# Gated DeltaNet stage: full 128-wide products in the first five merge levels, and decay differences built on VectorE

## The chip, the cores and the metric

The kernel runs on one core of one Trainium2 chip. The metric is the device time of one execution in microseconds (us); a smaller number is better.

## The reference

One layer of a hybrid encoder over two token groups (1024 and 512 tokens, together 1536 tokens in 12 tiles of 128), model width 1024. The part that matters here is the second of three mixers, a bidirectional gated DeltaNet with 4 heads of width 128:

```python
g = jnp.cumsum(g, axis=-1)
decay = jnp.exp(jnp.where(incl, g[..., :, None] - g[..., None, :], -jnp.inf))
k_beta = k * beta[..., None]
a_mat = jnp.einsum("bhnid,bhnjd->bhnij", k_beta, k) * jnp.where(strict, decay, 0.0)
sol = lax.linalg.triangular_solve(eye + a_mat, rhs, left_side=True, lower=True, unit_diagonal=True)
qk = jnp.einsum("bhnid,bhnjd->bhnij", q, k) * decay
...
v_new = u_c - jnp.einsum("bhck,bhkv->bhcv", w_c, s)
s = s * jnp.exp(gl_c)[..., None] + jnp.einsum("bhck,bhcv->bhkv", kd_c, v_new)
```

Both directions are computed. Around it stand an input projection, neighbourhood attention, an RG-LRU, a gated merge and a squared-relu MLP, all in float32.

## The kernel before

`trunk` runs its stages one after another; `deltanet` is one of them. It works through the 4 heads in order. In each head the kernel uses chunks of 128 tokens and handles them in six **units**: `UN` lists them as (token block of four tiles, direction), so a unit is four 128x128 matrices, a tile of 128x512. Every engine has its own program, and they meet only at the named semaphores in `S`. VectorE is `dve`, ScalarE `act`, GpSimd `pool`, TensorE `pe`, SyncE `sp`. A head goes through three parts.

**The decay part.** For each of the six units ScalarE builds two tiles of `dd` from the decay row `gbc` and the per-token column `col` (L1304 to L1315): eight activations of 128x128 (relu of row minus column, and of column minus row), then two exponentials of 128x512. GpSimd multiplies both by a triangular mask (`decays`, L1244). VectorE then turns the Gram products in PSUM into `am` (L1613, four instructions of 128x128) and `qk` (L1616, one of 128x512); before each it scales two tiles to token order (`token_major`, L1625), and twice in a head it multiplies `qd` by the queries (L1638). `dd` has two pairs of tiles, so ScalarE waits before unit n until `amat` of unit n-2 is done. TensorE makes the Gram products of one token block at a time (L1428), and those of the next block wait until VectorE has read those of the last. When the sixth unit is done, TensorE transposes `am` into `at` (L1441).

**The level loop.** The triangular inverse is built by merging diagonal blocks, seven levels (`LEVELS`) over six units. The first level is a masked copy. The other six make 36 steps (`NS`) on TensorE: step s issues the first product of s (S: `at` by `tn`, L1457 or L1460), the second product of s-2 (U: `sbuf_s` by `un`, L1471 or L1474) and a transpose of s-4 (T: L1490). ScalarE copies S out of PSUM (L1336 or L1338) and T (L1326); VectorE merges U under a mask into `un` (L1654). In the first 30 steps, those below `SMALL`, the blocks being merged lie in the two 64-row diagonal quadrants. There each 128x128 product is made as two of 64 columns, one for each quadrant, placed in the array by `tile_position`; the ScalarE copy is in two halves too. The last six steps are full products. Between these steps the engines do the next head's convolution, norms and scaling (`front`, at fixed unit numbers) and the last head's output (`OUT_AT`). The next S of a unit waits for its transposed tile to be copied (`t_ev`), and TensorE keeps program order.

**The chain.** Eight sequential steps over the tokens of a head update the state `st` (L1500 to L1515, L1682 to L1686).

Of the kernel before, what the change touches and what calls it, by code (L numbers as in the profile page):

```python
# [17 lines left out]
ACT = mybir.ActivationFunctionType  # L18
ALU = mybir.AluOpType
AX = mybir.AxisListType  # L20

P = 128
# [4 lines left out]
NT = T // P  # L27
TB = 512
NTB = T // TB
# [1065 lines left out]
NS = UNITS - 2 * NTB  # L1095
# [4 lines left out]
def deltanet(nc, proj, g_rows, cols, masks, o_t, conv_w, norm_w, ident, ones):  # L1100
# [9 lines left out]
    UN = [(tg, d) for tg in range(NTB) for d in range(2)]  # L1110
    with Space(nc, "dn") as s:
# [5 lines left out]
        S = {x: s.sem(x) for x in names}  # L1117
# [16 lines left out]
        nw = s.sb("nw", [1])  # L1134
        col = s.sb("col", [4, NT])
        cx = s.sb("cx", [6, NT])
        ncol = s.sb("ncol", [2, NT])
        ms, rr, rs = (s.sb(v, [2, NT]) for v in ("ms", "rr", "rs"))
        oms, orr, ors = (s.sb(v, [NT]) for v in ("oms", "orr", "ors"))
        st = s.sb("st", [4, P])  # L1140
# [14 lines left out]
        def glast(d):  # L1155
            g4 = gbc[:, d].rearrange("p (t n) -> p t n", n=P)
            return g4[:, :, P - 1] if d == 0 else g4[:, :, 0]

        SMALL = NS - 2 * NTB
        halves = (slice(0, 64), slice(64, P))  # L1160

        def live_chains(step):
            return [(j, d, SEG[g][0] // P + (step if d == 0 else SEG[g][1] // P - 1 - step))
# [103 lines left out]
        def _(act):  # L1267
# [29 lines left out]
            def main(i, more):  # L1297

                act.wait_ge(S["cols_in"], i + 1)
                act.activation(flat(cx[:]), flat(cx[:]), ACT.Exp).then_inc(S["cexp"], 1)  # L1300
                act.wait_ge(S["g_in"], i * 32 + 32)
                for d in range(2):
                    act.activation(qd[:, d], gbc[:, d], ACT.Exp).then_inc(S["eg"], 1)
                for n, (tg, d) in enumerate(UN):  # L1304
                    b = n % 2
                    if n >= 2:
                        act.wait_ge(S["amat"], i * 12 + 2 * (n - 2) + 2)
                    for sign, a, bias in ((1.0, 2 * b, ncol), (-1.0, 2 * b + 1, col)):
                        for j in range(4):
                            t = 4 * tg + j  # L1310
                            act.activation(dd[:, a, j], gbc[:, d, t * P:(t + 1) * P], ACT.Relu, bias=bias[:, d, t:t + 1],
                                           scale=sign).then_inc(S["ediff"], 1)
                    for a in (2 * b, 2 * b + 1):
                        act.wait_ge(S["ediff"], i * 48 + 8 * n + 4 + 4 * (a - 2 * b))
                        act.activation(flat(dd[:, a]), flat(dd[:, a]), ACT.Exp, scale=-1.0).then_inc(S["dexp"], 1)  # L1315

                act.wait_ge(S["scaled"], i * 6 + 6)
                act.copy(kf[:], yn[:, 1]).then_inc(S["kc"], 1)
                for n in range(2 * NTB):
                    act.wait_ge(S["u_mm"], i * VT + n + 1)  # L1320
                    act.copy(at[:, n], ps[:, 4 + 2 * (n % 2)]).then_inc(S["at_ev"], 1)

                def turned(k):

                    act.wait_ge(S["t_mm"], i * NTR + k + 1)
                    act.copy(tn[:, k % 6], ps[:, 4 + 2 * (k % 2)]).then_inc(S["t_ev"], 1)  # L1326

                for k in range(NS):
                    act.wait_ge(S["s_mm"], i * NS + k + 1)
                    if k == 0:  # L1330
                        act.wait_ge(S["amat"], i * 12 + 12)
                    if k >= 4:
                        act.wait_ge(S["u_mm"], i * VT + 6 + k - 3)
                    if k < SMALL:
                        for r in halves:
                            last = act.copy(sbuf_s[k % 4][r, :, r], ps[r, k % 2, :, r])  # L1336
                    else:
                        last = act.copy(sbuf_s[k % 4], ps[:, k % 2])  # L1338
                    last.then_inc(S["s_ev"], 1)
                    if T_LAG <= k < NTR + T_LAG:  # L1340
                        turned(k - T_LAG)
                    u = k + 2 * NTB
                    if i and u == OUT_AT["squares"]:
                        out_squares(i - 1)
                    if i and u == OUT_AT["root"]:
                        out_root(i - 1)
                    if more:
                        front(i + 1, u)
                    if u == ZTANH_AT:
                        act.wait_ge(S["z_in"], i * 16 + 16)  # L1350
                        act.activation(th[:, 1], zt, ACT.Tanh, scale=0.5).then_inc(S["zt"], 1)

                act.wait_ge(S["stored"], i * 16 + 16)
                for step in range(8):
                    for j, d, t in live_chains(step):
                        act.wait_ge(S["new_mm"], i * 24 + K_OF[(step, j)] + 1)
                        if step:
                            act.wait_ge(S["st_mm"], i * 24 + K_OF[(step - 1, j)] + 1)
                        act.copy(nb[:, j], ps[:, 4 + j, 0]).then_inc(S["new_ev"], 1)
                    for j, d, t in live_chains(step):  # L1360
                        act.wait_ge(S["o_mm"], i * 24 + K_OF[(step, j)] + 1)
                        act.copy(oc[d][:, t * P:(t + 1) * P], ps[:, 4 + j, 1]).then_inc(S["o_ev"], 1)
                if not more:
                    out_squares(i)
                    out_root(i)
# [7 lines left out]
        def _(pe):  # L1373
# [29 lines left out]
            def main(i, more):  # L1403
# [40 lines left out]
                for step in range(NS + T_LAG):  # L1444
                    if step < NS:
                        k, n = step, step % 6

                        if k < 6:
                            pe.wait_ge(S["u_ev"], i * VT + k + 1)
                        else:  # L1450
                            pe.wait_ge(S["t_ev"], i * NTR + k - 5)
                        if k >= 2:
                            pe.wait_ge(S["s_ev"], i * NS + k - 1)
                        for j in range(4):
                            if k < SMALL:
                                for r in halves:
                                    last = pe.matmul(ps[r, k % 2, j, r], at[:, n, j, r], tn[:, n, j, r], start=True, stop=True,  # L1457
                                                     tile_position=(0, r.start))
                            else:
                                last = pe.matmul(ps[:, k % 2, j], at[:, n, j], tn[:, n, j], start=True, stop=True)  # L1460
                        last.then_inc(S["s_mm"], 1)
                    if U_LAG <= step < NS + U_LAG:
                        k = step - U_LAG
# [2 lines left out]

                        pe.wait_ge(S["u_ev"], i * VT + 6 + k - 1)
                        for j in range(4):
                            if k < SMALL:
                                for r in halves:  # L1470
                                    last = pe.matmul(ps[r, 5 + 2 * (k % 2), j, r], sbuf_s[k % 4][:, j, r], un[:, n, j, r], start=True,  # L1471
                                                     stop=True, tile_position=(0, r.start))
                            else:
                                last = pe.matmul(ps[:, 5 + 2 * (k % 2), j], sbuf_s[k % 4][:, j], un[:, n, j], start=True, stop=True)  # L1474
                        last.then_inc(S["u_mm"], 1)
                        if i and 6 + k == OUT_AT["lengths"]:
                            out_lengths(i - 1)
# [50 lines left out]
        def _(dve):  # L1528
# [64 lines left out]
            def main(i, more):  # L1593
# [2 lines left out]

                c.link(dve.tensor_copy(col[:], cols[:, bass.ds(i, 1)].rearrange("p a k t -> p (a k) t")))
                dve.wait_ge(S["g_in"], i * 32 + 32)
                c.add(dve.tensor_scalar(ncol[:], col[:, 0:2], -1.0, None, ALU.mult))
                for d in range(2):  # L1600
                    c.add(dve.tensor_copy(cx[:, d], col[:, d]))
                    c.add(dve.tensor_tensor(cx[:, 2 + d], glast(d), col[:, d], ALU.subtract))
# [1 line left out]
                c.wait()  # L1604
                dve.sem_inc(S["cols_in"], 1)

                def amat(n):
                    tg, d = UN[n]
                    b = n % 2
                    dve.wait_ge(S["dmask"], i * 12 + 2 * n + 2)  # L1610
                    dve.wait_ge(S["gram"], i * NTB + tg + 1)
                    for j in range(4):
                        last = dve.scalar_tensor_tensor(am[:, n, j], ps[:, 0, j], col[:, 2 + d, 4 * tg + j:4 * tg + j + 1],  # L1613
                                                        dd[:, 2 * b, j], ALU.mult, ALU.mult)
                    last.then_inc(S["amat"], 1)
                    dve.tensor_tensor(qk[:, n], ps[:, 1], dd[:, 2 * b + 1], ALU.mult).then_inc(S["amat"], 1)  # L1616

                def token_major(n):
# [3 lines left out]
                    for d in range(2):  # L1622
# [2 lines left out]
                        dve.tensor_tensor(dst[:, d, 4 * tg:4 * tg + 4], ps[:, 4 + n % 4], fac.unsqueeze(2).to_broadcast([P, 4, P]),  # L1625
                                          ALU.mult).then_inc(S["kt_ev"], 1)

                dve.wait_ge(S["cexp"], i + 1)

                c.link(dve.scalar_tensor_tensor(cx[:, 0:2], col[:, 2:4], -1.0, cx[:, 0:2], ALU.mult, ALU.mult))  # L1630

                dve.wait_ge(S["scaled"], i * 6 + 6)
                for n in range(2 * NTB):
                    token_major(n)
                    if n % 3 == 1:
                        d = n // 3
                        dve.wait_ge(S["eg"], i * 2 + d + 1)
                        dve.tensor_tensor(qd[:, d], qd[:, d], yn[:, 0], ALU.mult).then_inc(S["qd"], 1)  # L1638
                    amat(n)
# [69 lines left out]
        if _step < SEG[_g][1] // P:  # L1709
            K_OF[(_step, _j)] = len(K_OF)  # L1710
K_FRONT = len(CONV_AT) + 1
K_DN = 1 + 7 + 1


def merge_project(nc, proj, o_t, w_br, w_out, x_tm, under_x, rows):
# [636 lines left out]
```

## Time and profile before

| | |
|---|---|
| runs | 3393.93 us median of 3 (3393.69 to 3394.67) |
| the profiled execution | 3393.69 us |
| its span in the profile | 3391.9 us |
| busy, share of the span | PE 92%, PEld 75%, DVE 37%, ACT 34%, POOL 34% |
| mean granted TensorE clock | 0.953 |
| the DeltaNet stage | about 1245 to 1960 us of the span |

The times of a row are from the start of the span. PE is the matmul side of TensorE and PEld its weight loads, which run beside the matmuls. A float32 matmul shows as two records on each; a transpose shows as one. The start of one group of PEld records to the start of the next is the time in which TensorE issued the group. DVE is VectorE, ACT ScalarE, POOL GpSimd. A granted clock of 1.00 is 2.4 GHz, 0.50 is 1.2 GHz. Busy times overlap a little where an engine pipelines: an instruction's record can end after the next has begun.

### The profile page before, as it was taken

The page shows a single profiled execution, that of the slowest core. Times are in us where ns is not written, and L with a number is a line of the kernel's source. Part 1 is how long each engine was busy: PE and PEld are TensorE (multiplying, and loading weights), DVE is VectorE, ACT ScalarE, POOL GpSimd, SP SyncE. Part 2 cuts the span into 40 slices and gives each one's busy share as a digit, 9 for nine tenths or more (in the row PEclk, how much of TensorE's full clock was granted, in tenths as well). Part 3 has the DMA queues.
Part 4 walks back from the last instruction along what each step waited for, and adds up shares of the span by engine and source line. Part 5 has one row for each costly group of instructions (what it writes and reads, how often), then busy time and mean ns, then how long its engine had stood idle before and what let it go on. Part 6 is the DMA issues. An engine that isn't in the chain of part 4 may idle for free. (4 is left out here: it accounts for less than half of the span.)

```text
span 3391.9 us, 44853 instructions
## 1 busy us (share of the span) xinstructions
PE 3118.0 (92%) x18195; PEld 2556.8 (75%) x18195; DVE 1262.6 (37%) x1955; ACT 1149.6 (34%) x2003; POOL 1167.7 (34%) x761
## 2 busy tenths in 40 slices
PE   6999999999998966969696889998999999999998
PEld 4788887878887544858585768786888888888887
DVE  4242323221100787576755423412223323232323
ACT  3221213141111655565656421223233333333222
POOL 4211111111111202121212034245666666656664
PEclk8999999999999987979797989998999999999999
DMA  3533232433421741001000064433332333323331
GB/s 103 176 134 109 72 106 93 130 101 112 135 87 64 254 134 48 20 29 39 29 20 1 20 204 167 146 120 118 99 94 93 100 100 97 118 84 100 100 124 62
DMA packets 235963, 334.30 MB, mean 99 GB/s; under 512 B 32368, under 2 KB 185712, under 8 KB 235760
## 3 DMA queue, kind: packets, MB, share of 16 engines
q1 hardware_dynamic: 235760, 331.44, 30.4%
q8 instruction: 146, 2.39, 0.3%
q14 instruction: 57, 0.47, 0.0%
HBM read 254.27 MB, written 86.93 MB: 101 GB/s over the span
## 5 line engine op out<-in xcount | busy, mean ns | idle before, releaser
L102 PE MATMUL pj_acc<-u_hi,pj_w_hi 128*128 128x512 f32 x1464 | 583.1, 398 | 15.1 <-POOL u_lo L488 13.3
L104 PE MATMUL pj_acc<-u_hi,pj_w_lo 128*128 128x512 f32 x1464 | 571.8, 391 | 0.0
L103 PE MATMUL pj_acc<-u_lo,pj_w_hi 128*128 128x512 f32 x1464 | 571.7, 390 | 0.0
L2269 DVE TENSOR_TENSOR x_tm<-m_ps,x_tm 128x512 f32<-128x512 f32 x384 | 265.0, 691 | 745.3 <-PE m_ps L104 745.3
L482 POOL TENSOR_TENSOR pj_w_lo<-pj_w_raw,pj_w_hi 128x1024 fp32r<-128x1024 f32 x61 | 148.2, 2430 | 826.7 <-ACT pj_w_hi L512 826.7
L102 PEld LDWEIGHTS pj_acc<-u_hi,pj_w_hi 128*128 128x128 f32 x1464 | 276.0, 188 | 78.3 <-POOL u_lo L488 14.2
L2146 POOL TENSOR_TENSOR m_w_lo<-m_w_raw,m_w_hi 128x1024 fp32r<-128x1024 f32 x96 | 237.9, 2498 | 262.7 <-ACT m_w_hi L2060 262.7
L103 PEld LDWEIGHTS pj_acc<-u_lo,pj_w_hi 128*128 128x128 f32 x1464 | 276.1, 189 | 62.0 <-issue 5.7
L104 PEld LDWEIGHTS pj_acc<-u_hi,pj_w_lo 128*128 128x128 f32 x1464 | 275.8, 188 | 57.7
L102 PE MATMUL m_ps<-m_v_hi,m_w_hi 128*128 128x512 f32 x768 | 300.1, 391 | 2.4 <-DVE m_v_lo L2237 2.4
L103 PE MATMUL m_ps<-m_v_lo,m_w_hi 128*128 128x512 f32 x768 | 299.8, 390 | 0.0
L104 PE MATMUL m_ps<-m_v_hi,m_w_lo 128*128 128x512 f32 x768 | 299.7, 390 | 0.0
L102 PE MATMUL m_ps<-m_w_hi,m_h_hi 128*128 128x512 f32 x768 | 299.5, 390 | 0.0
L104 PE MATMUL m_ps<-m_w_hi,m_h_lo 128*128 128x512 f32 x768 | 298.8, 389 | 0.0
L103 PE MATMUL m_ps<-m_w_lo,m_h_hi 128*128 128x512 f32 x768 | 298.8, 389 | 0.0
L2139 POOL TENSOR_TENSOR m_w_lo<-m_w_raw,m_w_hi 128x1024 fp32r<-128x1024 f32 x96 | 227.6, 2391 | 22.4 <-ACT m_w_hi L2053 22.4
L1878 POOL TENSOR_TENSOR mo_w_lo<-mo_w_raw,mo_w_hi 128x512 fp32r<-128x512 f32 x72 | 94.4, 1310 | 336.9 <-ACT mo_w_hi L1845 336.9
L512 ACT CAST pj_w_hi<-pj_w_raw 128x1024 fp32r<-128x1024 f32 x61 | 64.0, 1049 | 404.7 <-PE pj_acc L104 392.1
L2072 ACT CAST m_h_hi<-m_rel 128x512 fp32r<-128x512 f32 x96 | 59.8, 623 | 356.4 <-POOL m_rel L2152 356.4
L2060 ACT CAST m_w_hi<-m_w_raw 128x1024 fp32r<-128x1024 f32 x96 | 96.4, 1052 | 247.1 <-PE m_ps L104 247.1
L102 PEld LDWEIGHTS m_ps<-m_v_hi,m_w_hi 128*128 128x128 f32 x768 | 144.8, 189 | 32.9 <-DVE m_v_lo L2237 2.8
L103 PEld LDWEIGHTS m_ps<-m_v_lo,m_w_hi 128*128 128x128 f32 x768 | 144.9, 189 | 30.2
(261 smaller groups left out, 5419.2 us busy)
## 6 DMA issues: line engine op xcount, KB each, us to landing
m_w_raw<-in_w_mlp_dram SPq DMA_DIRECT2D x48, 1024.0 KB, 5.4
m_w_raw<-in_w_mlp_dram SPq DMA_DIRECT2D x96, 512.0 KB, 3.6
proj<-pj_stage SPq DMA_DIRECT2D x61, 768.0 KB, 3.4
pj_w_raw<-in_w_in_dram SPq DMA_DIRECT2D x61, 512.0 KB, 4.7
mo_gate<-proj SPq DMA_DIRECT2D x24, 768.0 KB, 4.3
mo_w_raw<-in_w_out_dram SPq DMA_DIRECT2D x48, 256.0 KB, 2.6
rpb_bias<-pj_shut SPq DMA_DIRECT2D x48, 192.0 KB, 3.0
rpb_bias<-rpb_near SPq DMA_DIRECT2D x24, 384.0 KB
```

The costliest lines, as they stand in the source:

```text
L102: pe.matmul(out, w_hi, x_hi, start=first, stop=False)
L103: pe.matmul(out, w_hi, x_lo, start=False, stop=False)
L104: return pe.matmul(out, w_lo, x_hi, start=False, stop=last)
L482: pool.tensor_tensor(w_lo[:, n % 2], w_raw[:, n % 2], w_hi[:, n % 2].bitcast(F32), ALU.subtract).then_inc(lo_done, 1)
L512: act.copy(w_hi[:, n % 2], w_raw[:, n % 2]).then_inc(hi_done, 1)
L1878: pool.tensor_tensor(w_lo[:, sl % 2], w_raw[:, sl % 3], w_hi[:, sl % 2].bitcast(F32), ALU.subtract).then_inc(w_lo_done, 1)
L2060: act.copy(w2_hi[:, (2 * gg + j) % 4], w2_raw[:, j]).then_inc(w2_hi_done, 1)
L2072: act.copy(h_hi[:, m % 4], rel[:, j]).then_inc(hh_done, 1)
L2139: pool.tensor_tensor(w1_lo[:, m % 4], w1_raw[:, :, j * P:(j + 1) * P], w1_hi[:, m % 4].bitcast(F32), ALU.subtract).then_inc(w1_lo_done, 1)
L2146: pool.tensor_tensor(w2_lo[:, m % 4], w2_raw[:, j], w2_hi[:, m % 4].bitcast(F32), ALU.subtract).then_inc(w2_lo_done, 1)
L2269: dve.tensor_tensor(xt, ps2[:, q % 4], xt, ALU.add).then_inc(added, 1)
```

## The change

Two edits, both in `deltanet`.

The first takes `SMALL` and `halves` away: in the first 30 steps of the level loop S and U are made as full 128x128 products, four for a unit instead of eight of 64 columns, without `tile_position`, and ScalarE copies the whole 128x512 tile in one instruction.

The second moves the decay differences. ScalarE keeps the two exponentials. VectorE gets a function `ediff(n)`: one subtraction of 128x512 (row minus column, broadcast), a minimum with zero into the second tile, a maximum with zero in place in the first. It is called for unit n+1 ahead of `token_major(n)` and `amat(n)`. The first half of `amat` becomes two 128x512 multiplications, the second waiting for the first, where four 128x128 instructions stood. `ncol` goes.

```diff
-                    for sign, a, bias in ((1.0, 2 * b, ncol), (-1.0, 2 * b + 1, col)):
-                        for j in range(4):
-                            t = 4 * tg + j
-                            act.activation(dd[:, a, j], gbc[:, d, t * P:(t + 1) * P], ACT.Relu, bias=bias[:, d, t:t + 1],
-                                           scale=sign).then_inc(S["ediff"], 1)
-                    for a in (2 * b, 2 * b + 1):
-                        act.wait_ge(S["ediff"], i * 48 + 8 * n + 4 + 4 * (a - 2 * b))
-                        act.activation(flat(dd[:, a]), flat(dd[:, a]), ACT.Exp, scale=-1.0).then_inc(S["dexp"], 1)
+                    act.activation(flat(dd[:, 2 * b]), flat(dd[:, 2 * b]), ACT.Exp, scale=-1.0).then_inc(S["dexp"], 1)
+                    act.activation(flat(dd[:, 2 * b + 1]), flat(dd[:, 2 * b + 1]), ACT.Exp).then_inc(S["dexp"], 1)
...
-                    if k < SMALL:
-                        for r in halves:
-                            last = act.copy(sbuf_s[k % 4][r, :, r], ps[r, k % 2, :, r])
-                    else:
-                        last = act.copy(sbuf_s[k % 4], ps[:, k % 2])
-                    last.then_inc(S["s_ev"], 1)
+                    act.copy(sbuf_s[k % 4], ps[:, k % 2]).then_inc(S["s_ev"], 1)
...
-                            if k < SMALL:
-                                for r in halves:
-                                    last = pe.matmul(ps[r, k % 2, j, r], at[:, n, j, r], tn[:, n, j, r], start=True, stop=True,
-                                                     tile_position=(0, r.start))
-                            else:
-                                last = pe.matmul(ps[:, k % 2, j], at[:, n, j], tn[:, n, j], start=True, stop=True)
+                            last = pe.matmul(ps[:, k % 2, j], at[:, n, j], tn[:, n, j], start=True, stop=True)
...
-                            if k < SMALL:
-                                for r in halves:
-                                    last = pe.matmul(ps[r, 5 + 2 * (k % 2), j, r], sbuf_s[k % 4][:, j, r], un[:, n, j, r], start=True,
-                                                     stop=True, tile_position=(0, r.start))
-                            else:
-                                last = pe.matmul(ps[:, 5 + 2 * (k % 2), j], sbuf_s[k % 4][:, j], un[:, n, j], start=True, stop=True)
+                            last = pe.matmul(ps[:, 5 + 2 * (k % 2), j], sbuf_s[k % 4][:, j], un[:, n, j], start=True, stop=True)
...
+                def ediff(n):
+                    tg, d = UN[n]
+                    b = n % 2
+                    if n >= 2:
+                        dve.wait_ge(S["amat"], i * 12 + 2 * (n - 2) + 2)
+                    e = dd[:, 2 * b]
+                    c.link(dve.tensor_tensor(e, four(gbc[:, d, tg * TB:(tg + 1) * TB]),
+                                             col[:, d, 4 * tg:4 * tg + 4].unsqueeze(2).to_broadcast([P, 4, P]), ALU.subtract))
+                    dve.tensor_scalar(dd[:, 2 * b + 1], e, 0.0, None, ALU.min).then_inc(S["ediff"], 1)
+                    dve.wait_ge(S["ediff"], i * 12 + 2 * n + 1)
+                    dve.tensor_scalar(e, e, 0.0, None, ALU.max).then_inc(S["ediff"], 1)
...
-                    for j in range(4):
-                        last = dve.scalar_tensor_tensor(am[:, n, j], ps[:, 0, j], col[:, 2 + d, 4 * tg + j:4 * tg + j + 1],
-                                                        dd[:, 2 * b, j], ALU.mult, ALU.mult)
-                    last.then_inc(S["amat"], 1)
+                    c.link(dve.tensor_tensor(am[:, n], ps[:, 0], dd[:, 2 * b], ALU.mult))
+                    dve.tensor_tensor(am[:, n], am[:, n], col[:, 2 + d, 4 * tg:4 * tg + 4].unsqueeze(2).to_broadcast([P, 4, P]),
+                                      ALU.mult).then_inc(S["amat"], 1)
                     dve.tensor_tensor(qk[:, n], ps[:, 1], dd[:, 2 * b + 1], ALU.mult).then_inc(S["amat"], 1)
...
+                ediff(0)
                 dve.wait_ge(S["cexp"], i + 1)
...
                 for n in range(2 * NTB):
+                    if n + 1 < 2 * NTB:
+                        ediff(n + 1)
                     token_major(n)
```

## Rows read from the trace of the kernel before

**Rows 1.** The page, part 1: busy time of each engine.
```profile
PE 3118.0 (92%) x18195; PEld 2556.8 (75%) x18195; DVE 1262.6 (37%) x1955; ACT 1149.6 (34%) x2003; POOL 1167.7 (34%) x761
```

**Rows 2.** Windows: the 30 narrow level steps of heads 1, 3; sum of all four.
```profile
core 0: us, PE busy (x) PEld busy (x) DVE busy (x) ACT busy (x) POOL busy (x), PEclk, DMA share, GB/s
...
1494.70:1563.80 69.10, 64.67 (x1114) 54.98 (x1115) 53.10 (x66) 50.89 (x99) 6.98 (x2) 0.91 0.20 59
...
1831.00:1889.10 58.10, 54.96 (x1063) 46.74 (x1064) 27.57 (x39) 41.70 (x91) 0.00 (x0) 0.94 0.09 30
sum 256.50, PE 242.54 PEld 206.46 DVE 179.93 ACT 189.74 POOL 20.94; mean PE 60.64 PEld 51.61 DVE 44.98 ACT 47.44 POOL 5.24
```

**Rows 3.** Timeline, head 0, a narrow level step; start, length, engine, line.
```profile
1366.87 0.55 PEld L1457 LDWEIGHTS dn_ps<-dn_tn,dn_at 128*64 128x64 f32 x16 [0.17 <-issue]
1367.33 0.55 PEld L1471 LDWEIGHTS dn_ps<-dn_un,dn_dd 128*64 128x64 f32 x16
1367.60 0.75 ACT L1336 COPY dn_dd<-dn_ps 64x256 f32<-64x256 f32 x2
1367.95 0.42 PEld L1490 LDWEIGHTS dn_ps<-ident,dn_un 128*128 128x128 f32 x4
...
1368.54 0.55 PEld L1457 LDWEIGHTS dn_ps<-dn_tn,dn_at 128*64 128x64 f32 x16 [0.17 <-issue]
```

**Rows 4.** Timeline, full products: a step of head 3, a ScalarE copy of head 0.
```profile
1893.18 0.97 PEld L1460 LDWEIGHTS dn_ps<-dn_tn,dn_at 128*128 128x128 f32 x8
1894.07 0.97 PEld L1474 LDWEIGHTS dn_ps<-dn_un,dn_dd 128*128 128x128 f32 x8
1894.96 0.47 PEld L1490 LDWEIGHTS dn_ps<-ident,dn_un 128*128 128x128 f32 x4
1895.40 0.97 PEld L1460 LDWEIGHTS dn_ps<-dn_tn,dn_at 128*128 128x128 f32 x8
...
1402.09 0.59 ACT L1338 COPY dn_dd<-dn_ps 128x512 f32<-128x512 f32 x1 [0.31 <-PE dn_ps L1460]
```

**Rows 5.** Groups of weight loads, narrow steps of head 1: busy, mean | idle before, releasers.
```profile
L1457 PEld LDWEIGHTS dn_ps<-dn_tn,dn_at 128*64 128x64 f32 x480 | 18.8, 154 | 8.2 <-issue 4.1 <-ACT dn_tn L1326 3.1 <-ACT dn_at L1321 1.1
L1471 PEld LDWEIGHTS dn_ps<-dn_un,dn_dd 128*64 128x64 f32 x448 | 17.5, 153 | 0.9 <-ACT dn_dd L1336 0.9
L1401 PEld LDWEIGHTS dn_ps<-dn_am,ones 128*128 128x128 f32 x6 | 0.9, 188 | 1.7 <-DVE dn_am L1580 1.5
```

**Rows 6.** Timeline, decay part of head 1.
```profile
1453.20 1.26 ACT L1311 ACTIVATE dn_dd<-dn_gbc,dn_ncol 128x128 f32<-128x128 f32 x4
1455.54 1.14 ACT L1315 ACTIVATE dn_dd<-dn_dd 128x512 f32<-128x512 f32 x2
1457.98 1.27 POOL L1244 TENSOR_TENSOR dn_dd<-dn_dd,incl 128x512 f32<-128x512 f32 x1
1459.28 1.13 DVE L1613 SCALAR_TENSOR_TENSOR dn_am<-dn_ps,dn_col,dn_dd 128x128 f32<-128x128 f32 x4 [7.20 <-POOL dn_dd L1244]
1460.32 0.68 DVE L1616 TENSOR_TENSOR dn_qk<-dn_ps,dn_dd 128x512 f32<-128x512 f32 x1
1465.94 3.60 PE L1428 MATMUL dn_ps<-dn_yn 128*128 128x128 f32 x16 [2.57 <-DVE dn_qk L1616]
...
1482.90 0.68 DVE L1616 TENSOR_TENSOR dn_qk<-dn_ps,dn_dd 128x512 f32<-128x512 f32 x1
```

**Rows 7.** Timeline, head 1: GpSimd masks beside a VectorE multiplication of two SBUF tiles.
```profile
1474.98 1.27 POOL L1244 TENSOR_TENSOR dn_dd<-dn_dd,neg_strict 128x512 f32<-128x512 f32 x1 [3.00 <-ACT dn_dd L1315]
1475.30 2.56 DVE L1638 TENSOR_TENSOR dn_qd<-dn_qd,dn_yn 128x1536 f32<-128x1536 f32 x1
1476.21 2.79 POOL L1244 TENSOR_TENSOR dn_dd<-dn_dd,incl 128x512 f32<-128x512 f32 x1
```

**Rows 8.** Groups on VectorE in the DeltaNet stage, shapes apart.
```profile
L1545 DVE SCALAR_TENSOR_TENSOR dn_yn<-dn_x,dn_cw,dn_yn 128x512 f32<-128x512 f32 x36 | 26.8, 746 | 0.3
L1543 DVE TENSOR_SCALAR dn_yn<-dn_x,dn_cw 128x512 f32<-128x512 f32 x12 | 6.0, 501 | 0.1
```

More of the change, by code:

```diff
@@ L1136, in deltanet @@
         cx = s.sb("cx", [6, NT])
-        ncol = s.sb("ncol", [2, NT])
         ms, rr, rs = (s.sb(v, [2, NT]) for v in ("ms", "rr", "rs"))
@@ L1157, in glast @@
             return g4[:, :, P - 1] if d == 0 else g4[:, :, 0]
-        SMALL = NS - 2 * NTB
-        halves = (slice(0, 64), slice(64, P))
         def live_chains(step):
@@ L1303, in main @@
                     act.activation(qd[:, d], gbc[:, d], ACT.Exp).then_inc(S["eg"], 1)
-                for n, (tg, d) in enumerate(UN):
+                for n in range(2 * NTB):
+                    act.wait_ge(S["ediff"], i * 12 + 2 * n + 2)
                     b = n % 2
-                    if n >= 2:
-                        act.wait_ge(S["amat"], i * 12 + 2 * (n - 2) + 2)
-                    for sign, a, bias in ((1.0, 2 * b, ncol), (-1.0, 2 * b + 1, col)):
-                        for j in range(4):
-                            t = 4 * tg + j
-                            act.activation(dd[:, a, j], gbc[:, d, t * P:(t + 1) * P], ACT.Relu, bias=bias[:, d, t:t + 1],
-                                           scale=sign).then_inc(S["ediff"], 1)
-                    for a in (2 * b, 2 * b + 1):
-                        act.wait_ge(S["ediff"], i * 48 + 8 * n + 4 + 4 * (a - 2 * b))
-                        act.activation(flat(dd[:, a]), flat(dd[:, a]), ACT.Exp, scale=-1.0).then_inc(S["dexp"], 1)
+                    act.activation(flat(dd[:, 2 * b]), flat(dd[:, 2 * b]), ACT.Exp, scale=-1.0).then_inc(S["dexp"], 1)
+                    act.activation(flat(dd[:, 2 * b + 1]), flat(dd[:, 2 * b + 1]), ACT.Exp).then_inc(S["dexp"], 1)
                 act.wait_ge(S["scaled"], i * 6 + 6)
@@ L1598, in main @@
                 dve.wait_ge(S["g_in"], i * 32 + 32)
-                c.add(dve.tensor_scalar(ncol[:], col[:, 0:2], -1.0, None, ALU.mult))
                 for d in range(2):
@@ L1711 @@
 K_FRONT = len(CONV_AT) + 1
-K_DN = 1 + 7 + 1
+K_DN = 1 + 6 + 1 + 2 * 6
 def merge_project(nc, proj, o_t, w_br, w_out, x_tm, under_x, rows):
```

## The prediction

> **What bounds the kernel now.** I read the page's busy times first. TensorE is busy for 92% of the span and VectorE and ScalarE for about a third [rows 1], but the change touches one stage, so that average decides nothing. I therefore went to windows of the DeltaNet stage. In the narrow level steps of the four heads, together 256.5 us, PE is busy 242.5 us, DVE 180 and ACT 190 [rows 2]. The reader is to see that TensorE paces these steps even in head 3, where DVE has little to do (27.6 us of 58.1). The timeline shows how. In an undisturbed step S starts at 1366.87, U at 1367.33, T at 1367.95 and the next S at 1368.54: 0.46 + 0.62 + 0.59 = 1.67 us [rows 3]. Nothing is waited for but 0.17 us called issue. Then I read what TensorE waits for inside such a window. In head 1 it is 3.1 us for ScalarE's copies of transposes, 0.9 for its copies of S, 1.5 for VectorE [rows 5]. That is 5.5 us of 69.1, so there is little slack to hide longer matmuls in.
>
> The decay part has another limit. TensorE is hardly used, and the part ends when VectorE finishes the sixth `qk`. In head 1 that is 1482.90 + 0.68 = 1483.58 [rows 6]. Which wait ends last varies: the first unit waits for ScalarE, then GpSimd (DVE idle 7.20 us); the third waits for the Gram products, which themselves wait for VectorE's second `qk`.
>
> **The change, part by part. Full products in 30 steps.** The price stands in the trace, since the last steps of each head already have this form. S at 1893.18, U at 1894.07, T at 1894.96, next S at 1895.40 give 0.89 + 0.89 + 0.44 = 2.22 us [rows 4]. Against 1.67 that is +0.43 for S, +0.27 for U and -0.15 for T, in all +0.55 us a step. U and T cost less extra than S because the pause when TensorE goes between the narrow and the full form (the 0.17 before S, the same amount hidden in U's 0.62) goes away. The Trainium skill, TensorEngine Tiling (Array Packing), Key Properties, says that changing the mode drains the array; if those drains were the larger part, the full form would win, but the rows make them 0.33 us a step against 0.86 us of array time, so the trace decides against it.
>
> Steps 4 to 29 have all three parts: 26 x 0.55 = 14.3 us. Steps 0 to 3 have four S and two U and no transposes between: 6 x 0.43 = 2.6. Steps 30 and 31 only turn a narrow U into a full one, 0.1 each (0.27 less the 0.15 on T): 0.2. A head pays 17.1 us, four heads 68.4. What can give some back is the waiting in [rows 5]: it comes from ScalarE or VectorE being late after one long instruction, and a longer step lets them catch up. Head 1 has 5.5 us of it. I credit a bit over half, 3 us a head, 12 in all. The level loop then costs **+56 us**; ends are 50 (nearly all of 5.5 back in each head, less in those with less) and 68 (nothing back).
>
> ScalarE's two half copies take 0.75 us, the whole tile 0.59 [rows 3, 4]. The 0.16 us saved is ScalarE time, and ScalarE does not pace the loop, so I take it as nothing; what worth it has is in the credit. The mean granted clock in these windows is 0.91 to 0.94 [rows 2], so stretches at the lower of its two levels occur. While a stretch at half clock keeps its length it loses the same time whatever is issued in it, so I price the added matmuls at the full clock.
>
> **Decay differences on VectorE.** ScalarE loses eight activations a unit. Four take 1.26 us [rows 6], so about 2.4 us a unit. VectorE gains, for a unit, one subtraction of two SBUF tiles, with a wait at its end, about 0.71 us (nearest: 0.68 for one 128x512 with an operand in PSUM [rows 6], 0.75 for one of two SBUF tiles [rows 8]); a minimum, waited for, and a maximum: 0.50 alone [rows 8], 0.90 for both with their overlap. That makes 1.6 us. `amat` was 1460.32 - 1459.28 = 1.04 us for four pieces [rows 6] and becomes 0.71 + 0.62 = 1.33. So VectorE gets 1.9 us a unit, 11.4 a head, against idle time of the same size in this part. The order must be followed.
>
> I do this for head 1, from 1450.1 where VectorE starts `ediff(0)`. ScalarE is busy with `qd` until 1453.20 [rows 6], so its exponentials of unit 0 end at 1454.4. GpSimd takes 1.22 us a mask, both are done at 1457.0. VectorE's unit then is ediff 1.6, `token_major` 1.2, `amat` with `qk` 1.93, and twice `qd` 1.6. Without any interference: amat(0) 1457.0 to 1458.9, ediff(2) and the rest until amat(1) ends at 1465.3; the Gram products take 3.8 us at the lower clock (1465.94, 3.60 [rows 6]), so amat(2) runs 1469.1 to 1471.1; amat(3) ends at 1475.8; again Gram, amat(4) ends at 1482.2, amat(5) at 1485.3. That is **+1.7 us** a head: VectorE's new work mostly falls into the waits for ScalarE and for the Gram products.
>
> But there is interference. The VectorE multiplication at 1475.30 took 2.56 us where the same size two SBUF tiles alone would need about 1.65. GpSimd's mask had started 0.32 us before it and ran until 1476.25; 1476.25 + 1.6 = 1477.86, where it ended. GpSimd's next mask, put at 1476.21, took 2.79 us instead of 1.27: it ended 1.14 us after VectorE [rows 7]. So the two were done one after the other. The Trainium skill, SBUF — State Buffer, Who interferes with whom, gives the rule: VectorE instructions with two SBUF inputs, and tensor_scalar in its two-port mode, hold a port pair that GpSimd needs, and the later one waits for the whole of the earlier one. By that rule the subtraction, minimum, maximum and second half of `amat` would all be exposed, and the trace agrees for the one kind of VectorE instruction it shows.
>
> The four new kinds of instruction of each unit stand just where the masks run. Going through the same order with that rule of one after the other, read from [rows 7]: amat(0)'s second half waits 0.5 us for the mask of unit 1, ediff(2) then 0.7; in later units the second half waits 0.2 to 0.6 for the first mask and ediff 0.6 to 0.7 for the second, which itself was pushed back by VectorE. amat(1) ends at 1467.2, amat(3) at 1479.35, amat(5) at 1490.1: **+6.5 us** a head. I take 6, since the interplay at single waits is a guess: 4 x 6 = **+24 us**; ends 7 (no blocking) and 36 (each unit blocked once more, 0.4 us).
>
> `ncol` going away is a 24-column instruction, too small to count. SyncE's load of the next head's `gbc` waits for `amat` to finish and so starts some 6 us later, under a level loop of over 60 us that follows it. The chain part, and every other stage, is untouched.
>
> **Sum.** 3393.7 us (the profiled execution's own time, 1.8 us around its span of 3391.9 and 0.2 below the median of the runs) + 56 + 24 = 3474 us.
>
> **The rivals.** *No blocking between VectorE and GpSimd.* The new instructions are short, and the row that shows the blocking is of a long one. Then the decay part costs 7 us and the time is 3394 + 56 + 7 = 3457 us. For it: broadcast operands of 4 columns might not count as an SBUF tile. Against: both instructions in [rows 7] are clearly stretched.
>
> *Nothing is caught up.* The waits of [rows 5] come from ScalarE's long instructions at fixed places and could stay. Then 68 + 24 and some more low clock, 3 to 7 us, give about 3490 us. Against: a late ScalarE has 0.55 us more in every step and 0.16 us less to do.
>
> *TensorE does not set the pace, ScalarE's copies do (faster).* If the step were paced by S, its copy, U, merge, T, its copy, the array time would be hidden, and 0.16 us in each of 120 steps, 19 us, would be gained: 3394 - 19 + 7 = 3382 us. It decides only where ScalarE's share of a step exceeds 2.22 us; it is busy 190 us in 120 steps, 1.6 a step [rows 2], and the narrow steps repeat at 1.67 with every gap named.
>
> *No change to speak of.* This would need the added 68 us of array time to hide almost whole, with 5.5 us of wait a head to hide it in.
>
> **How the numbers follow.** My forecast gets 0.53, no blocking 0.24, nothing caught up 0.16, more than 3500 us 0.02, faster 0.03, and no change 0.02. A change of under 0.2% (7 us) is about what a measurement of this kernel cannot tell from none. The range runs from the low ends of both parts, 50 + 7, to the high ends, 68 + 36: 3451 to 3498 us. It leaves out the faster and the unchanged case, the one above 3500, and a tenth or so beyond the bounds of the two parts. Slower 0.95, same 0.02, faster 0.03.
>
> **What the profile of the changed kernel would show.** The undisturbed level step repeats at 2.2 us without the 0.17 us of issue; 3 us or more there at full clock would be a new wait. The narrow-step windows grow by 12 to 17 us a head, and the waits for ScalarE's transposes shrink below 3 us. In the decay part the masks or the `ediff` instructions are stretched beyond 1.27 and 0.75 us; if they are not, the no-blocking case holds. The first `amat` starts about 2 us earlier than now, the last ends later. The prediction is wrong if the part before the first transposes of `am` gets shorter, or if the step stays below 2 us.

## The result and the profile after

The changed kernel takes 3469.6 us (median of 4 runs, 3467.2 to 3469.7) against 3394.3 us before. The ratio is 1.022 with a 95% interval of 1.0207 to 1.0233: slower by 75 us. The forecast was 3474 us. The profiled execution took 3468.34 us around a span of 3466.6.

To place the time I cut each head at four points of the trace: the start of VectorE's copy of `col`, the end of the sixth `qk`, the start of the first matmul record of S, and the start of the last one. The decay part lies between the first two, the level loop between the last two. Summed over the four heads, the decay part went from 141.6 to 160.9 us (+19.4) and the level loop from 309.0 to 364.4 us (+55.4). Together that is 74.8 us, and the span grew by 74.7; every other piece moved by less than 2 us either way.

The page's busy times (part 1) and the windows of the 30 level steps, answering to [rows 1, 2]:

```profile
PE 3187.0 (92%) x16275; PEld 2654.2 (77%) x16275; DVE 1314.3 (38%) x1975; ACT 1073.4 (31%) x1691; POOL 1180.3 (34%) x761
...
core 0: us, PE busy (x) PEld busy (x) DVE busy (x) ACT busy (x) POOL busy (x), PEclk, DMA share, GB/s
...
1518.60:1600.20 81.60, 81.19 (x650) 77.89 (x651) 53.14 (x66) 45.82 (x69) 6.98 (x2) 0.93 0.16 50
...
sum 310.80, PE 309.47 PEld 299.98 DVE 179.88 ACT 170.78 POOL 20.94; mean PE 77.37 PEld 75.00 DVE 44.97 ACT 42.70 POOL 5.24
```

The reader is to see that PE is now busy in 309.5 of 310.8 us, with almost nothing left between its matmuls, while ScalarE has 19 us less to do and VectorE the same. Head by head these windows are 12.6 to 15.7 us longer than before, within the 12 to 17 that the prediction gave. The page alone hides this: PE's share of the whole span is 92% in both kernels, and the number of records fell by over four thousand.

The timeline of weight loads, one step of head 0, answers to [rows 3]:

```profile
1363.27 0.97 PEld L1439 LDWEIGHTS dn_ps<-dn_tn,dn_at 128*128 128x128 f32 x8
1364.16 0.97 PEld L1448 LDWEIGHTS dn_ps<-dn_un,dn_dd 128*128 128x128 f32 x8
1365.05 0.47 PEld L1464 LDWEIGHTS dn_ps<-ident,dn_un 128*128 128x128 f32 x4
1365.49 0.64 PEld L1439 LDWEIGHTS dn_ps<-dn_tn,dn_at 128*128 128x128 f32 x5
```

S, U and T are issued 0.89, 0.89 and 0.44 us apart: 2.22 us, and no idle time in front of S. The groups of head 1, answering to [rows 5], say what TensorE still waits for there:

```profile
L1439 PEld LDWEIGHTS dn_ps<-dn_tn,dn_at 128*128 128x128 f32 x241 | 32.2, 209 | 1.2 <-ACT dn_at L1310 1.1
L1448 PEld LDWEIGHTS dn_ps<-dn_un,dn_dd 128*128 128x128 f32 x224 | 29.0, 202 | 0.0
L1464 PEld LDWEIGHTS dn_ps<-ident,dn_un 128*128 128x128 f32 x104 | 12.7, 145 | 2.9 <-issue 2.7 <-DVE dn_un L1641 0.2
L1385 PEld LDWEIGHTS dn_ps<-dn_am,ones 128*128 128x128 f32 x6 | 1.1, 238 | 0.5 <-DVE dn_am L1554 0.5
```

The 3.1 us for ScalarE's transposes and the 0.9 for its S copies are gone. Of VectorE's 1.5, 0.5 is left, and a new wait of 0.2 for `dn_un` has come. So head 1 waits 0.7 us where it waited 5.5; over the four heads such waits in the 30 steps, without the one ahead of the first S, fell from 17.8 to 2.6 us.

In the decay part, the timeline of head 1 (answering to [rows 6, 7]) shows the new instructions beside GpSimd's masks:

```profile
1475.53 0.69 DVE L1597 TENSOR_TENSOR dn_am<-dn_ps,dn_dd 128x512 f32<-128x512 f32 x1 [2.05 <-POOL dn_dd L1240]
1476.25 1.01 DVE L1598 TENSOR_TENSOR dn_am<-dn_am,dn_col 128x512 f32<-128x512 f32 x1
1476.67 1.71 POOL L1240 TENSOR_TENSOR dn_dd<-dn_dd,incl 128x512 f32<-128x512 f32 x1
1477.18 0.68 DVE L1600 TENSOR_TENSOR dn_qk<-dn_ps,dn_dd 128x512 f32<-128x512 f32 x1
1477.90 1.03 DVE L1586 TENSOR_TENSOR dn_dd<-dn_gbc,dn_col 128x512 f32<-128x512 f32 x1
...
1489.46 1.26 POOL L1240 TENSOR_TENSOR dn_dd<-dn_dd,incl 128x512 f32<-128x512 f32 x1
1489.66 1.61 DVE L1598 TENSOR_TENSOR dn_am<-dn_am,dn_col 128x512 f32<-128x512 f32 x1
```

Alone, `amat`'s second half takes 0.69 us. It takes 1.01 where it starts late in a mask, and 1.61 where it starts 0.2 us behind the start of one. The mask that follows is stretched to 1.71. `qk`, which reads PSUM, takes 0.68 whatever GpSimd does. The groups of the whole stage, shapes apart, give the means over all 24 of each kind:

```profile
L1598 DVE TENSOR_TENSOR dn_am<-dn_am,dn_col 128x512 f32<-128x512 f32 x24 | 25.6, 1067 | 0.8
L1586 DVE TENSOR_TENSOR dn_dd<-dn_gbc,dn_col 128x512 f32<-128x512 f32 x24 | 21.1, 878 | 1.3
L1588 DVE TENSOR_SCALAR dn_dd<-dn_dd 128x512 f32<-128x512 f32 x24 | 10.2, 426 | 0.8
L1240 POOL TENSOR_TENSOR dn_dd<-dn_dd,neg_strict 128x512 f32<-128x512 f32 x24 | 42.1, 1753 | 70.8 <-ACT dn_dd L1304 70.8
```

### The profile page after: what moved, and what is told of

It is laid out like the page before. It is cut to its first block and busy times, and to the rows that moved or that the text cites. A ratio compares the mean times of both kernels' runs of the same rounds, so it can differ in the third digit from the quotient of the medians.

```text
span 3466.6 us, 40721 instructions
## 1 busy us (share of the span) xinstructions
PE 3187.0 (92%) x16275; PEld 2654.2 (77%) x16275; DVE 1314.3 (38%) x1975; ACT 1073.4 (31%) x1691; POOL 1180.3 (34%) x761
## 5 line engine op out<-in xcount | busy, mean ns | idle before, releaser
L482 POOL TENSOR_TENSOR pj_w_lo<-pj_w_raw,pj_w_hi 128x1024 fp32r<-128x1024 f32 x61 | 148.0, 2427 | 826.3 <-ACT pj_w_hi L512 826.3
L104 PEld LDWEIGHTS m_ps<-m_v_hi,m_w_lo 128*128 128x128 f32 x768 | 144.7, 188 | 30.2
```

Of the source, the lines that this page charges most:

```text
L104: return pe.matmul(out, w_lo, x_hi, start=False, stop=last)
L482: pool.tensor_tensor(w_lo[:, n % 2], w_raw[:, n % 2], w_hi[:, n % 2].bitcast(F32), ALU.subtract).then_inc(lo_done, 1)
```

## The experiments

All were timed against the kernel before. In the table, "decay" and "level" are the sums of the two parts over four heads, read from each kernel's profile as above.

| kernel | time, us | before it, us | ratio, 95% interval | decay | level |
|---|---|---|---|---|---|
| before | | | | 141.6 | 309.0 |
| the change | 3469.6 | 3394.3 | 1.0207 to 1.0233 | 160.9 | 364.4 |
| level_only | 3446.0 | 3394.3 | 1.0137 to 1.0168 | 141.2 | 363.3 |
| decay_only | 3414.7 | 3394.3 | 1.0043 to 1.0076 | 160.9 | 312.0 |
| amat_only | 3405.7 | 3394.3 | 1.0020 to 1.0046 | 152.3 | 310.3 |
| ediff_only | 3400.8 | 3395.4 | 1.0010 to 1.0029 | 147.4 | 310.9 |
| nomask_before | 3388.8 | 3395.1 | 0.9973 to 0.9992 | 135.7 | 309.3 |
| nomask_decay | 3401.0 | 3395.1 | 1.0010 to 1.0028 | 148.0 | 310.4 |
| whole_copy | 3389.1 | 3395.1 | 0.9972 to 0.9992 | 141.3 | 306.6 |
| narrow_transpose | 3380.7 | 3394.3 | 0.9946 to 0.9975 | 141.1 | 298.3 |
| reorder | 3377.7 | 3395.4 | 0.9930 to 0.9960 | 122.1 | 312.7 |
| reorder_narrow | 3366.2 | 3395.4 | 0.9895 to 0.9932 | 122.1 | 298.0 |

The level sum of a kernel whose level loop is untouched lies between 309 and 313 us. It goes with the time at the lower granted clock, 0.50: in these loops that was 40.7 us in the kernel before (309.0) and 48.2 and 48.6 in decay_only and reorder (312.0 and 312.7). The decay sum repeats to half a microsecond. What lies outside the two parts differs from the kernel before by up to 4 us either way between profiled executions, so the sums of the parts say more of an edit than the medians do.

**level_only: the full products alone.** The diff is the level half of the change, and nothing else:

```diff
-                    if k < SMALL:
-                        for r in halves:
-                            last = act.copy(sbuf_s[k % 4][r, :, r], ps[r, k % 2, :, r])
...
+                    act.copy(sbuf_s[k % 4], ps[:, k % 2]).then_inc(S["s_ev"], 1)
```

> Only the full products of the level loop; the decay part is that of before. If the two edits act on separate parts and add up: +55 us against before (3449 us), the step repeats at 2.22 us and the decay part of head 1 stays at 35.6 us. Rival, that the edits lean on each other (the longer level loop gives the decay part more slack, or the other way round): below +45 or above +65 us.

Measured: +51.7 us by the medians, +54.4 in the level loop of the profile, and a decay part as before. The rival falls. With decay_only the medians add up to 51.7 + 20.4 = 72.1 us, where the change costs 75.3; the parts in the profiles add up better, 54.4 + 19.3 = 73.7 against 74.8.

**decay_only: the decay differences alone.** The diff is the other half of the change (`ediff`, the two-step `amat`, ScalarE's loop cut to its exponentials), with `SMALL` and `halves` kept.

> Only the decay differences on VectorE; the level loop keeps its narrow products. Additive theory: +20 us against before (3414 us), 5 us a head, all between the first instruction of a head on VectorE and its last qk. Rival, that the relief of ScalarE is worth something elsewhere: below +12 us.

Measured: +20.4 us; the decay part of heads 1 to 3 is 40.8, 40.8 and 39.9 us against 35.6, 35.8 and 35.8. The eight activations a unit taken from ScalarE gave back nothing elsewhere.

**amat_only: only the two-step `amat`, on the kernel before.**

```diff
-                    for j in range(4):
-                        last = dve.scalar_tensor_tensor(am[:, n, j], ps[:, 0, j], col[:, 2 + d, 4 * tg + j:4 * tg + j + 1],
-                                                        dd[:, 2 * b, j], ALU.mult, ALU.mult)
-                    last.then_inc(S["amat"], 1)
+                    c.link(dve.tensor_tensor(am[:, n], ps[:, 0], dd[:, 2 * b], ALU.mult))
+                    dve.tensor_tensor(am[:, n], am[:, n], col[:, 2 + d, 4 * tg:4 * tg + 4].unsqueeze(2).to_broadcast([P, 4, P]),
+                                      ALU.mult).then_inc(S["amat"], 1)
```

> Of the decay edit only its smallest piece: amat as two multiplications of 128x512, the second of two SBUF tiles; the differences stay on ScalarE. If the blocking between VectorE and GpSimd and the added VectorE time cost only where VectorE paces the part: 0.3 us a unit and 0.3 to 0.9 us of blocking in some, of which the idle time of the part absorbs most: +2 to +8 us in all. Rival, that amat carries most of the 20 us of the decay edit: +12 us or more.

Measured: +11.4 us, +10.7 in the decay part. This missed my range and nearly met the rival's. The timeline of its head 1 shows why:

```profile
1470.26 0.68 DVE L1612 TENSOR_TENSOR dn_am<-dn_ps,dn_dd 128x512 f32<-128x512 f32 x1
...
1470.97 1.41 DVE L1613 TENSOR_TENSOR dn_am<-dn_am,dn_col 128x512 f32<-128x512 f32 x1
...
1472.30 0.68 DVE L1615 TENSOR_TENSOR dn_qk<-dn_ps,dn_dd 128x512 f32<-128x512 f32 x1
...
1473.02 1.28 ACT L1311 ACTIVATE dn_dd<-dn_gbc,dn_ncol 128x128 f32<-128x128 f32 x4 [2.52 <-DVE dn_qk L1615]
```

From the first half to `qk` it is 2.04 us, against 1.04 in [rows 6]: 0.3 for the longer form and 0.7 for the mask in its way. ScalarE and the Gram products wait for exactly this `qk`. The idle time that I had counted as cover lies elsewhere in VectorE's timeline; at this place there is none.

**ediff_only: the differences on VectorE, `amat` in four pieces as before.** The diff against decay_only is the one above, turned round.

> The decay differences on VectorE as in the change, but amat in the four 128x128 pieces of before; the level loop as before. With amat alone the decay part of heads 1 to 3 grew by 2.7 us, with both by 5.1 us. If the two pieces add up, the differences alone cost 2.4 us a head, about +10 us against before. Rival, that amat was dear only because it stretched the loop over ScalarE, which the change does not have: the differences alone cost 4 us a head or more, +16 us.

Measured: +5.5 us by the medians, +5.9 in the decay part, 1.4 to 1.6 us a head. It is below both expectations. So the larger new piece of VectorE's work, 1.6 us a unit, costs a quarter of a microsecond a unit: most of it stands in idle time, and ScalarE's eight activations no longer stand ahead of its exponentials. How much each of the two contributes, no run here separates. Apart, the two pieces cost 10.7 + 5.9 = 16.6 us, together 19.3: the last 2.7 us arise only with both.

**nomask_before and nomask_decay: GpSimd without reads.** In the kernel before and in decay_only, the two triangular masks are left out of the computation. GpSimd fills a spare tile instead, for about the same time.

```diff
+        spare = s.sb("spare", [2, 1312])
...
                     pool.wait_ge(S["dexp"], i * 12 + 2 * n + 2)
+                    pool.wait_ge(S["dmask"], i * 12 + 2 * n)
...
-                        pool.tensor_tensor(dd[:, a], dd[:, a], mask[:, d].unsqueeze(1).to_broadcast([P, 4, P]),
-                                           ALU.mult).then_inc(S["dmask"], 1)
+                        pool.memset(spare[:, a % 2], 0.0).then_inc(S["dmask"], 1)
```

> The kernel before with GpSimd's two masks of a unit left out of the computation; in their place GpSimd fills a spare tile of 1312 columns, about as long as a mask, reading nothing of SBUF. If GpSimd's time stays what it was, within 4 us of before (VectorE's own stretched qd products give back 0.5 to 1.5 us a head where they pace anything).

> The decay differences on VectorE (level loop as before), with the masks left out of the computation in the same way. Blocking theory: with GpSimd reading nothing, VectorE's subtraction takes 0.69 us and the second half of amat 0.69 us each time, and the edit costs about 7 us against the kernel with the masks left out, not 20. Rival, VectorE's added work by itself: 16 to 20 us as with the masks.

Measured: nomask_decay is 5.9 us above the kernel before by the medians, and 6.4 by the decay sums (148.0 less 141.6). But nomask_before is itself 6.3 us below it (5.9 in the decay sum), where I had expected up to 4 either way, so between the two the decay edit costs 12.2 us. That lies between my 7 and the rival's 16 for this pair. The 7 was worked out against the kernel before as it is, whose decay part already holds some blocking; set against that kernel it holds. The groups of nomask_decay, VectorE with shapes apart, show that the blocking was taken away entirely:

```profile
L1617 DVE TENSOR_TENSOR dn_am<-dn_am,dn_col 128x512 f32<-128x512 f32 x24 | 16.6, 692 | 0.8
L1605 DVE TENSOR_TENSOR dn_dd<-dn_gbc,dn_col 128x512 f32<-128x512 f32 x24 | 16.6, 692 | 1.3
L1616 DVE TENSOR_TENSOR dn_am<-dn_ps,dn_dd 128x512 f32<-128x512 f32 x24 | 16.4, 685 | 11.4 <-POOL dn_spare L1245 7.4 <-PE dn_ps L1421 4.0
...
L1245 POOL MEMSET dn_spare<- 128x1312 f32 x48 | 55.8, 1192 | 73.9 <-ACT dn_dd L1308 73.4
```

The subtraction and the second half of `amat` are at 692 ns, where they had means of 878 and 1067, and GpSimd's filling stands at 1192 ns, not 1581 and 1753. GpSimd was at work at the same places, and what is gone is its reading. A fill is also some 0.07 us shorter than a mask that nothing disturbs (1.27 us), so a small part of the gain is that: the first `amat` of head 1 waits 6.99 us in nomask_before and 7.20 before. In nomask_before the decay part is 1.4 to 1.5 us a head shorter, mostly because `qd` and the masks block one another in the kernel before too [rows 7]: the eight `qd` multiplications took 2.13 or 2.56 us there and 1.75 here.

**whole_copy: one ScalarE copy of S, products narrow as before.** The diff is the ScalarE hunk of level_only alone.

> The kernel before with the S tile copied by one ScalarE instruction of 128x512 (0.59 us) in place of two halves (0.75 us); products unchanged. If TensorE paces the level loop: 0 to -6 us against before, the part of the waits for a late ScalarE that 0.16 us a step can catch up. Rival, ScalarE paces the loop: about 0.16 x 120 = -19 us.

Measured: -6.1 us by the medians with an interval of -2.7 to -9.5 us, and -2.4 in the level loop of the profile. That loop had 45.2 us at the lower clock where the kernel before had 40.7, so 2.2 us more were lost to the clock. TensorE's waits for other engines in the narrow steps fell from 17.8 to 13.1 us. About 3 us of the gain lie outside the level loop, where the edit changes nothing and executions differ by as much. The rival's -19 is out: ScalarE does not pace the loop.

**narrow_transpose: no change of form within a step.** On whole_copy, the transposes of k = 2 to 23 in each head become narrow products with the identity.

```diff
+                            if 2 <= k < SMALL - 2 * NTB:
+                                for r in halves:
+                                    last = pe.matmul(ps[r, 4 + 2 * (k % 2), j, r], un[:, n, j, r], ident[:, r], start=True, stop=True,
+                                                     tile_position=(0, r.start))
+                            else:
+                                last = pe.transpose(ps[:, 4 + 2 * (k % 2), j], un[:, n, j], ident[:])
```

> The level loop of before, with the transposes of most narrow steps made as eight 64-column products with the identity, so that TensorE stays in the narrow form for the whole step, and with the S tile copied whole. If the pauses between the forms are what the rows say (0.33 us a step): the step falls from 1.67 to about 1.4 us where nothing else is late, in 22 steps a head, and with ScalarE then close to the pace some of it is lost: -10 to -24 us against before. Rival, that the pause is not of the change of form but of the transposes' own operands: no step below 1.6 us, and no change or slower.

Measured: -13.5 us, and -10.7 in the level loop, with as much time at the lower clock as before (40.8 us); against whole_copy the loop is 8.3 us shorter. The timeline of its weight loads, head 0:

```profile
1348.35 0.55 PEld L1452 LDWEIGHTS dn_ps<-dn_tn,dn_at 128*64 128x64 f32 x16
1348.81 0.55 PEld L1466 LDWEIGHTS dn_ps<-dn_un,dn_dd 128*64 128x64 f32 x16
1349.28 0.55 PEld L1487 LDWEIGHTS dn_ps<-ident,dn_un 128*64 128x64 f32 x16
1349.75 0.26 PEld L1452 LDWEIGHTS dn_ps<-dn_tn,dn_at 128*64 128x64 f32 x6
```

The step is 0.46 + 0.47 + 0.47 = 1.40 us and the 0.17 us in front of S has gone. T has become no cheaper itself (sixteen records in 0.47 against four in 0.42), so the 0.27 us saved are the two pauses, 0.33 together, less 0.05 of the dearer T. The rival falls; the changed kernel says the same, where the transposes themselves are as they were and no pause stands in front of S. Of 22 x 0.27 x 4 = 24 us possible, less than half arrives. One reason is that TensorE now meets the engines that feed it sooner: its waits for them come to 21.3 us in the narrow steps, against 13.1 in whole_copy. The rest was not taken apart.

**reorder: two moves in the decay part.** On the kernel before.

```diff
-                for d in range(2):
-                    act.activation(qd[:, d], gbc[:, d], ACT.Exp).then_inc(S["eg"], 1)
...
+                    if n in (1, 3):
+                        act.activation(qd[:, n // 2], gbc[:, n // 2], ACT.Exp).then_inc(S["eg"], 1)
...
-                    if n % 3 == 1:
-                        d = n // 3
-                        dve.wait_ge(S["eg"], i * 2 + d + 1)
-                        dve.tensor_tensor(qd[:, d], qd[:, d], yn[:, 0], ALU.mult).then_inc(S["qd"], 1)
                     amat(n)
+                    if n in (1, 3):
+                        d = n // 2
+                        dve.wait_ge(S["eg"], i * 2 + d + 1)
+                        dve.tensor_tensor(qd[:, d], qd[:, d], yn[:, 0], ALU.mult).then_inc(S["qd"], 1)
```

> The kernel before with two moves and nothing else: ScalarE makes the exponentials of qd after units 1 and 3 and not before unit 0, and VectorE multiplies qd after amat of units 1 and 3, into the wait for the Gram products, and not before amat of units 1 and 4. If the decay part is bound by the round trip ScalarE, GpSimd, VectorE, TensorE, as its waits say: the first amat starts 2.8 us earlier, and the part falls from 35.6 to about 31 us a head, -14 to -20 us in all. Rival, that ScalarE's total work bounds it: no change.

Measured: -17.6 us; the decay part of heads 1 to 3 takes 30.86 us each, 19.5 us less over four heads. The timeline of head 1 shows the first `amat` waiting 4.44 us instead of 7.20, and VectorE's `qd` at its full speed of 1.75 us:

```profile
1454.19 1.13 DVE L1613 SCALAR_TENSOR_TENSOR dn_am<-dn_ps,dn_col,dn_dd 128x128 f32<-128x128 f32 x4 [4.44 <-POOL dn_dd L1244]
...
1459.21 1.75 DVE L1639 TENSOR_TENSOR dn_qd<-dn_qd,dn_yn 128x1536 f32<-128x1536 f32 x1
1459.79 2.30 POOL L1244 TENSOR_TENSOR dn_dd<-dn_dd,neg_strict 128x512 f32<-128x512 f32 x1 [2.25 <-ACT dn_dd L1313]
```

The blocking is still there, but this time VectorE came first and GpSimd waits, where there is time for it. The first `amat` starts 2.75 us earlier after the copy of `col`, which is the exponentials' move; the other 2.0 us of head 1's 4.7 go with the move of the multiplications. The two moves were not run apart.

**reorder_narrow: both improvements.**

> The reorder together with the narrow transposes and the whole S copy. The two act in separate parts of a head, so they should add: -14 for the one as measured and -14 to -20 for the other, 3360 to 3367 us. Rival, that they share slack (ScalarE): above 3372 us.

Measured: 3366.2 us (3358.4 to 3370.5), -29.1, a ratio of 0.9914. It beats the kernel before by 0.9% and the changed one by 3%. The two gains add up: the decay part is that of reorder (122.1 us) and the level loop that of narrow_transpose (298.0 against 298.3).

## Why the prediction was right, point by point

*The step from 1.67 to 2.22 us.* Right to the digit, since [rows 3, 4] held both forms at the same clock. That the pauses go with the narrow form, and that they are the smaller part, was shown by narrow_transpose. The Trainium skill (TensorEngine Tiling (Array Packing), Key Properties: changing the mode drains the array) says why there would be a pause at all; the runs agree with a pause, 0.33 us a step for two changes of form, and do not show what happens in it.

*The sum of the level loop, +56.* Measured +55.4 in the change and +54.4 alone. The price was 68.4 us and the credit for waits 12. By the profile the waits in the narrow steps fell by 15.2 us. But 15 of these waits stand where TensorE goes from T to S, and the 0.17 us pause falls into them (the shortest are 0.20 us), which the step's price had already counted as gained: 2.6 us that stand in both places. What was given back beyond the price is thus about 12.6 us, an estimate from the rows, and close to the credit. The other assumption was that stretches at the lower clock keep their length. The granted clock shows 40.7 us of them in the four loops before and 38.5 after. At the start of each head they cost more than the full-clock price: S of step 0 to S of step 3 took 3.6 to 3.8 us before and 5.7 to 6.4 after, +1.9 to +2.7 where the price had 1.7. As the total did not grow, the later steps lost that much less. 68.4 - 12.6 and 1.1 less for the clock make 54.7.

*ScalarE's shorter copy as nothing.* whole_copy puts it at -2.4 us in the loop, or 4.7 by the waits that fell away; either was inside the credit.

*The decay part, +24.* Measured +19.4. The working had two terms: VectorE's new order without blocking, +1.7 us a head against the kernel before, and the blocking, which made 6.5 of it and which I cut to 6. The first term was right: nomask_decay's head 1 takes 37.42 us against 35.59, +1.8. The second was mis-sized: from there to the change's 40.78 us it is 3.4 us, where 4.3 (4.8 in the worked order) was forecast. Four heads make 6.4 + 13.0 against 7 + 17. The order supposed that the subtraction waits 0.6 to 0.7 us for the rest of a mask in four of six units; in the trace it waits 0.34 in 13 of 24 cases, because GpSimd's second mask begins again right after the second half of `amat` and is further along when VectorE comes back. `amat`'s second half waits 0.3 to 0.9 us in 19 of 24, where 0.2 to 0.6 was supposed. The first term is also a difference of two things that the prediction did not name apart. Without blocking in either kernel the new work costs 3.1 us a head (12.2 over four). Of that 1.4 to 1.5 us comes back, because the kernel before loses them mostly to its stretched `qd`, and in the change `qd` takes 1.75 us in both places. The working had this in it, since it put `qd` at 1.6.

*Cover for `amat`.* The prediction let the added 0.3 us of `amat` vanish partly in idle time. amat_only and ediff_only say how it is shared: the small piece costs 10.7 us alone, the large one 5.9. The next exponentials and Gram products wait for the `qk` right behind `amat`, so what lengthens `amat` delays them; most of `ediff` delays nothing.

*Minimum and maximum exposed too.* Not shown for these two. They took 0.43 us in every case, but none of the 48 overlaps a mask: each stands behind a subtraction that ran or waited until the mask was over. That a `tensor_scalar` can be held up by GpSimd is in the trace of the kernel before all the same, at the start of a head:

```profile
1290.15 0.18 DVE L1599 TENSOR_SCALAR dn_ncol<-dn_col 128x24 f32<-128x24 f32 x1
...
1447.56 2.29 POOL L1229 COPY dn_un<-ident 128x512 f32<-128x512 f32 x4
1448.25 0.52 DVE L1599 TENSOR_SCALAR dn_ncol<-dn_col 128x24 f32<-128x24 f32 x1
1448.68 0.64 DVE L1601 COPY dn_cx<-dn_col 128x12 f32<-128x12 f32 x1
```

In head 0 no GpSimd copy runs there, and the small instructions take 0.16 to 0.18 us. In heads 1 to 3 they take 0.51 to 0.65 us as long as GpSimd's copies run. ScalarE's first exponential then starts 2.29 us behind the copy of `col` in head 1, and 0.95 us in head 0. That accounts for the 1.2 to 1.3 us by which the decay part of head 0 is shorter than the others in the kernel before (34.4 against 35.6 to 35.8 us). These are other instructions beside other GpSimd work; of the minimum and the maximum beside a mask no run tells.

*The rivals.* Without blocking would have been right only for nomask_decay. "Nothing is caught up" is refuted by the waits, of head 1 as of all four. ScalarE as the pace is refuted by whole_copy. The time came out between the 3457 us of the rival without blocking and the forecast.

## What to carry to other kernels

When a stage already contains both forms of an instruction, read the pitch of each from the start of one group to the start of the next, and add the pauses between forms: the sum over steps was 56 us where 54 to 55 were measured. On an engine with idle time, ask of each added instruction which wait it stands in: 1.6 us a unit of new VectorE work cost 0.25, while `amat`, longer by 0.3, cost 0.45 with its blocking, since the next units wait for the `qk` behind it. And look at what stands ahead of a wait: moving `qd`'s exponentials out of the way of the first unit, and its multiplications into the wait for the Gram products, gained 19.5 us in the decay part, as much as the decay edit costs there. Where two engines block one another, let the one that has time come second: behind `qd` at its full 1.75 us it was GpSimd's mask that took 2.30. How much of the 19.5 this order is worth was not run by itself.

## What the runs showed of the hardware

- A VectorE multiplication or subtraction of two SBUF tiles (128x512, 0.69 us alone) grew when it started during a GpSimd multiplication that reads SBUF, in the changed kernel in all 33 cases: once to 0.73, else to 1.01 to 1.62 us. It stayed at 0.69 in all 48 cases of nomask_decay, 28 of which overlap a GpSimd fill that only writes. One with an operand in PSUM stayed at 0.68 or 0.69 in both. The Trainium skill, SBUF — State Buffer, Who interferes with whom, says the same of two SBUF inputs against GpSimd's reads, and these runs agree.
- VectorE's `tensor_scalar` of 24 columns and copy of 12 columns took 0.51 to 0.65 us while GpSimd copied SBUF tiles of 128x512, and 0.16 to 0.18 alone.
- Two float32 products of 64 columns placed side by side are issued in 0.115 us (four pairs in 0.46), one full product in 0.22: half the issue time. A change between the forms costs about 0.16 us at the full clock; before S at the lower one the pause is 0.33 (seven cases in the kernel before, against 77 of 0.17 at the full clock).
- An ordinary product with the identity in the narrow form is nearly as quick as a transpose (0.47 against 0.42 us for four tiles), and saves both pauses.
